# Two sums of squares taken from high and low parts, with GpSimd making square and low part, and a chunk mask added into the bias tile

## The reference

```python
def rmsnorm(x, g):
    x32 = x.astype(jnp.float32)
    y = x32 * lax.rsqrt(jnp.mean(x32 * x32, axis=-1, keepdims=True) + EPS)
    return (y * g.astype(jnp.float32)).astype(x.dtype)

def first_block(x, ...):
        xr, yr, q, k, v, ga, gb = jnp.split(p, cuts, axis=-1)
        ...
        q = head_rmsnorm(q.reshape(b_, s_, ATT_HEADS, HEAD_DIM), q_norm_g[l])
        k = head_rmsnorm(k.reshape(b_, s_, ATT_HEADS, HEAD_DIM), k_norm_g[l])
        y_b = stick_breaking_attention(q, k, v)
        mix = jax.nn.sigmoid(ga) * y_a + jax.nn.sigmoid(gb) * y_b

def chunked_rel_attention(q, k, v, rel_bias):
    ...
    s = jnp.einsum('bcqhd,bckhd->bhcqk', qc, kb).astype(jnp.float32) * (hd ** -0.5) + bias[None, :, None]
    valid = (jnp.arange(nc)[:, None] - LEFT_CHUNKS + jnp.arange(BAND)[None, :]) >= 0
    s = jnp.where(valid[None, None, :, None, :], s, jnp.finfo(jnp.float32).min)
    p = jax.nn.softmax(s, axis=-1).astype(v.dtype)
```

## Time and profile before

| | |
|---|---|
| median of 3 runs | 1972.4 us (1970.75 to 1972.7) |
| the profiled execution, its own time | 1976.53 us |
| its span, from the first instruction to the last | 1974.7 us |
| mean granted clock of TensorE | 0.99 of full |
| busy: TensorE, its weight loads | 1929.9 us, 1570.2 us |
| busy: VectorE, ScalarE, GpSimd | 944.9 us, 916.9 us, 788.6 us |

### The profile page before, as it was taken

The page is one execution under the profiler, slowest core; times in us unless marked ns, Lnnn a source line. Parts: engine busy times, 40 slices in busy tenths (PEclk is TensorE's granted clock), DMA queues, the critical chain, the costliest instruction groups (busy, mean ns, idle before and its releaser), DMA issues.

```text
span 1974.7 us, 25379 instructions
## 1 busy us (share of the span) xinstructions
PE 1929.9 (98%) x8744; PEld 1570.2 (80%) x8744; DVE 944.9 (48%) x1135; ACT 916.9 (46%) x1220; POOL 788.6 (40%) x357
## 2 busy tenths in 40 slices
PE   6999999999999999999999999999999999999998
PEld 5778777877788888888888888787777788888886
DVE  6666666666443343222434331446776553434312
ACT  5577777776555554223222222356767332222222
POOL 0133333334344444443444445543332534444443
PEclk9999999999999999999999999999999999999999
DMA  7333333333222222222222223222222222222332
GB/s 302 116 99 126 127 127 124 120 106 128 75 96 96 96 96 96 97 98 90 99 96 96 96 98 104 90 81 86 74 74 75 78 94 96 96 96 96 100 102 75
DMA packets 54617, 203.17 MB, mean 103 GB/s; under 512 B 6064, under 2 KB 6192, under 8 KB 53296
## 3 DMA queue, kind: packets, MB, share of 16 engines
q1 hardware_dynamic: 54576, 202.62, 30.4%
HBM read 200.50 MB, written 2.10 MB: 103 GB/s over the span
## 4 chain that ended last, share of the span: by engine, by line
PE 76%; issue 12%; POOL 6%; DVE 3%; ACT 2%; DMA 0%; POOLq 0%; ACTq 0%; DVEq 0%
PE bank L617 23%; PE bank L618 22%; PE bank L622 22%; POOL WL L512 5%; PE bank L1034 1%; PE bank L641 1%; DVE TG L1627 1%; PE bank L823 1%; PE bank L824 1%; PE bank L828 0%; PE bank L1072 0%; PE bank L1063 0%; PE bank L767 0%; PE bank L775 0%; ACT ARENA L1540 0%
## 5 line engine op out<-in xcount | busy, mean ns | idle before, releaser
L512 POOL TENSOR_TENSOR WL<-ring,WH 128x1024 fp32r<-128x1024 f32 (+1 forms) x318 | 765.6, 2408 | 1146.4 <-ACT WH L1159 1146.4
L1159 ACT ACTIVATE WH<-ring 128x1024 fp32r<-128x1024 f32 (+2 forms) x326 | 338.9, 1042 | 830.2 <-PE bank L622 768.3
L617 PE MATMUL bank<-HH,WL 128*128 128x512 f32 x1744 | 689.1, 395 | 8.5 <-POOL WL L512 5.2
L618 PE MATMUL bank<-HH,WH 128*128 128x512 f32 x1744 | 683.0, 392 | 0.0
L622 PE MATMUL bank<-HL,WH 128*128 128x512 f32 x1744 | 432.5, 390 | 0.8 <-DVE HL L1627 0.8
L617 PEld LDWEIGHTS bank<-HH,WL 128*128 128x128 f32 x1744 | 330.1, 189 | 79.0 <-POOL WL L512 9.1
L618 PEld LDWEIGHTS bank<-HH,WH 128*128 128x128 f32 x1744 | 330.1, 189 | 67.4
L622 PEld LDWEIGHTS bank<-HL,WH 128*128 128x128 f32 x1744 | 327.4, 188 | 70.7 <-DVE HL L1627 2.8
L617 PE MATMUL bank<-FH,WL 128*128 128x512 f32 x544 | 211.8, 389 | 0.0
L618 PE MATMUL bank<-FH,WH 128*128 128x512 f32 x544 | 211.7, 389 | 0.0
L622 PE MATMUL bank<-FL,WH 128*128 128x512 f32 x544 | 135.0, 389 | 0.0
(11 more groups left out here) (345 smaller groups left out, 2082.5 us busy)
## 6 DMA issues: line engine op xcount, KB each, us to landing
ring<-in_stream SPq DMA_DIRECT2D x355, 512.0 KB, 3.3
ARENA<-in_ada SPq DMA_DIRECT2D x8, 1024.0 KB, 13.0
ring<-in_stream SPq DMA_DIRECT2D x8, 448.0 KB, 10.5
XT<-in_xt SPq DMA_DIRECT2D x2, 1024.0 KB, 6.1
result<-XT SPq DMA_DIRECT2D x3, 512.0 KB, 2.7
result<-XT SPq DMA_DIRECT2D x2, 256.0 KB, 2.1
vec<-in_vec SPq DMA_DIRECT2D x1, 220.0 KB, 2.6
```

The source lines that it names most:

```text
L512: nc.gpsimd.tensor_tensor(WL[:, slot, 0:cols], ring[:, u % RING, 0:cols], WH[:, slot, 0:cols].bitcast(F32), ALU.subtract).then_inc(w_low, 1)
L617: mm(out_ap, part(WL, base, loc, k), xh(k), start=(start and k == 0), stop=False)
L618: mm(out_ap, part(WH, base, loc, k), xh(k), start=False, stop=False)
L1159: A(WH[:, split_at(base, loc)[1], 0:cols], ring[:, u % RING, 0:cols], ACT.Copy).then_inc(w_high, 1)
```

## The change

The change has two parts.

In the first mixer's loop ScalarE now writes the square of the next q and k as fp32r (`QSH`, `KSH`), GpSimd squares the copies `QR` and `KR` once more in full precision and subtracts the high part (`QSL`, `KSL`), and TensorE sums high and low part with a matrix of -1 in fp32r; the root takes the sign back by its scale. `square_low` stands on GpSimd behind the split of GATES (q) and behind that of XR (k). The first head's sums, ahead of the loop, stay as they were.

In the second mixer the matmuls with `chunkb` are gone. GpSimd adds -1e30 to the later chunk's 64 columns of the bias tile in the ring, for queries 0 to 63 of each block, for both heads of a pair, ahead of the split of its unit 5.

Semaphores are merged or added to fit (`dt_act` takes the place of four).

```diff
@@ gpsimd, constants
-            keep(chunkb[:, :], ALU.is_ge, 0.0, [[0, P]], -1, base=63)
-            keep(chunkb[:, :], ALU.is_ge, 0.0, [[1, P]], 0, base=-64)
@@ gpsimd, first mixer
+            def square_low(h, square, x, low, high, done):
+                nc.gpsimd.tensor_tensor(M[square], M[x], M[x], ALU.mult).then_inc(done, 1)
+                pool.wait_ge(done, 2 * h + 1)
+                nc.gpsimd.tensor_tensor(M[low], M[square], M[high].bitcast(F32), ALU.subtract).then_inc(done, 1)
+
             with pool.Fori(0, HEADS - 1) as h:
                 for loc, n in HEAD_SPLIT.items():
                     split(U_HEAD, loc, SPLIT_BEFORE[U_HEAD] + n, h, HEAD_UNITS, 8, 2 * P if loc == GATES else UNIT)
+                    if loc == GATES:
+                        pool.wait_ge(q["q_evac"], 2 * h + 4)
+                        square_low(h, "QSQ", "QR", "QSL", "QSH", q["q_sq_low"])
+                    if loc == XR:
+                        pool.wait_ge(q["k_evac"], 2 * h + 4)
+                        square_low(h, "KSQ", "KR", "KSL", "KSH", q["k_sq_low"])
@@ gpsimd, second mixer
+            def mask_bias(t):
+                u = U_PAIR + BIAS
+                pool.wait_ge(arrived[u % RING], t * (16 * PAIR_UNITS // RING) + 16 * (u // RING + 1))
+                for hh in range(2):
+                    later_keys = ring[0:64, u % RING, (hh + 1) * S - 64:(hh + 1) * S]
+                    nc.gpsimd.tensor_tensor(later_keys, later_keys, chunk_mask[0:64, :], ALU.add).then_inc(r["bias_masked"], 1)
             with pool.Fori(0, 3) as t:
                 for j, loc in rest:
+                    if loc == 5:
+                        mask_bias(t)
                     split(U_PAIR, loc, SPLIT_BEFORE[U_PAIR] + 4 + j, t, PAIR_UNITS, 7)
@@ tensor
+            def square_parts(b, high, low, low_done, n):
+                mm(bank[b][:, :], negones_r[:, :], M[high], start=True, stop=False)
+                pe.wait_ge(low_done, 2 * n)
+                return mm(bank[b][:, :], negones_r[:, :], M[low], start=False, stop=True)
...
-                q_square(h + 1)
+                square_parts(5, "QSH", "QSL", q["q_sq_low"], h + 1).then_inc(q["q_ms"], 1)
                 pe.wait_ge(q["yb_done"], h + 1)
-                k_square(h + 1)
+                square_parts(7, "KSH", "KSL", q["k_sq_low"], h + 1).then_inc(q["k_ms"], 1)
...
-                        last = mm(bank[b][:, c + w - P:c + w], identb[:, :], chunkb[:, :], start=False, stop=True,
-                                  skip_group_check=True)
@@ scalar
-                A(M["RQ"], bank[5][:, :], ACT.Sqrt, bias=eps1[:, :], scale=1.0 / P).then_inc(q["rq_done"], 1)
+                A(M["RQ"], bank[5][:, :], ACT.Sqrt, bias=eps1[:, :], scale=sign / P).then_inc(q["rq_done"], 1)
...
-                A(M["QSQ"], bank[0][:, :], ACT.Square).then_inc(q["q_evac"], 1)
+                A(M["QSH"], bank[0][:, :], ACT.Square).then_inc(q["q_evac"], 1)
@@ vector
-                        dve.wait_ge(arrived[u % RING], t * (16 * PAIR_UNITS // RING) + 16 * (u // RING + 1))
+                        dve.wait_ge(r["bias_masked"], 2 * t + 2)
```

More of the change, by code:

```diff
@@ L224, in program @@
         strictb = sb("strictb", [P, P], BF16)
-        chunkb = sb("chunkb", [P, P], BF16)
+        chunk_mask = sb("chunk_mask", [P, 64])
         SS = sb("SS", [P, S])
@@ L247, in mixer1_tiles @@
             d.update(RSQ=d["RQ"], RSK=d["RK"], A2=d["M2"], ML=d["M2"], U=d["IX"])
+            d["QSH"], d["KSH"], d["QSL"], d["KSL"] = (tile_of(ML, n) for n in range(4))
             d["QN"], d["KN"], d["VF"] = (tile_of(QKV, n) for n in range(3))
@@ L380, in program @@
         SS_BEFORE = [0] + [8 + 6 * n for n in range(N_RES - 1)]
-        names = ("q_evac k_evac v_evac v_tr xr_evac q_ms k_ms rq_done rk_done rsq rsk qn_done kn_done "
+        names = ("q_evac k_evac q_sq_low k_sq_low v_evac v_tr xr_evac q_ms k_ms rq_done rk_done rsq rsk qn_done kn_done "
                  "gy_done conv_done z_done absz_done ez_done lnp_done p_done ph_done pl_done s_done att_done pv_done "
@@ L391, in program @@
         cv_dve = sem("cv_dve")
-        names = ("bc_conv bc_tap bc_silu dt_z dt_abs dt_exp dt_ln dt_sp dt_la cs_done tr_dt tr_evac "
-                 "g_mm g_evac g_mask xs_conv xs_tap xs_silu xs_tr xd_done sel_done csb_done "
+        names = ("bc_conv bc_tap bc_silu dt_act dt_sp dt_la cs_done tr_dt tr_evac "
+                 "g_mm g_evac g_mask bias_masked xs_conv xs_tap xs_silu xs_tr xd_done sel_done csb_done "
                  "dd_done ncst ed_done mm_done y_mm y_skip z_silu yz_done yss_done q_high q_low k_high k_low v_evac v_tr pv_mm "
@@ L496, in _ @@
             for t, value in ((ones, 1.0), (negones, -1.0), (negtri, -1.0), (ident, 0.0),
-                             (identb, 0.0), (strictb, NEG), (chunkb, NEG)):
+                             (identb, 0.0), (strictb, NEG), (chunk_mask, NEG)):
                 step(nc.gpsimd.memset(t[:, :], value))
@@ L533, in lows @@
                                             ALU.subtract).then_inc(pool_low, 1)
+            M = mixer1_tiles()
+            def square_low(h, square, x, low, high, done):
+                nc.gpsimd.tensor_tensor(M[square], M[x], M[x], ALU.mult).then_inc(done, 1)
+                pool.wait_ge(done, 2 * h + 1)
+                nc.gpsimd.tensor_tensor(M[low], M[square], M[high].bitcast(F32), ALU.subtract).then_inc(done, 1)
             pool.wait_ge(w_low, KD)
@@ L576, in _ @@
                 for j, loc in rest:
+                    if loc == 5:
+                        mask_bias(t)
                     split(U_PAIR, loc, SPLIT_BEFORE[U_PAIR] + 4 + j, t, PAIR_UNITS, 7)
             for j, loc in rest:
+                if loc == 5:
+                    mask_bias(3)
                 if loc == 11:
@@ L1046, in scores @@
                                    start=(i != 0), stop=False, skip_group_check=True)
-                        mm(bank[b][:, c:c + w], N[f"QB{hh}"][:, i * P:(i + 1) * P], N[f"KA{hh}"][:, 0:w],
-                           start=False, stop=False, skip_group_check=True)
+                        last = mm(bank[b][:, c:c + w], N[f"QB{hh}"][:, i * P:(i + 1) * P], N[f"KA{hh}"][:, 0:w],
+                                  start=False, stop=True, skip_group_check=True)
                         if hh and i == 3:
                             first.then_inc(unit_done, 1)
-                        last = mm(bank[b][:, c + w - P:c + w], identb[:, :], chunkb[:, :], start=False, stop=True,
-                                  skip_group_check=True)
                     last.then_inc(r["s_mm"], 1)
@@ L1241, in _, with q_root, k_root @@
             M = mixer1_tiles()
-            def q_root(n):
+            def q_root(n, sign=-1.0):
                 act.wait_ge(q["q_ms"], n + 1)
-                A(M["RQ"], bank[5][:, :], ACT.Sqrt, bias=eps1[:, :], scale=1.0 / P).then_inc(q["rq_done"], 1)
-            def k_root(n):
+                A(M["RQ"], bank[5][:, :], ACT.Sqrt, bias=eps1[:, :], scale=sign / P).then_inc(q["rq_done"], 1)
+            def k_root(n, sign=-1.0):
                 act.wait_ge(q["k_ms"], n + 1)
-                A(M["RK"], bank[7][:, :], ACT.Sqrt, bias=eps1[:, :], scale=1.0 / P).then_inc(q["rk_done"], 1)
+                A(M["RK"], bank[7][:, :], ACT.Sqrt, bias=eps1[:, :], scale=sign / P).then_inc(q["rk_done"], 1)
             def v_turned(n):
@@ L1269, in _ @@
             A(M["SGB"], bank[1][:, :], ACT.Sigmoid).then_inc(q["sgb_done"], 1)
-            q_root(0)
-            k_root(0)
+            q_root(0, 1.0)
+            k_root(0, 1.0)
             act.wait_ge(unit_done, DONE + KD)
@@ L1325, in _ @@
                 A(M["KR"], bank[1][:, :], ACT.Copy).then_inc(q["k_evac"], 1)
-                A(M["KSQ"], bank[1][:, :], ACT.Square).then_inc(q["k_evac"], 1)
+                A(M["KSH"], bank[1][:, :], ACT.Square).then_inc(q["k_evac"], 1)
                 absolute(h)
@@ L1477, in _ @@
             weight_high(U_BC, 6)
[L1478 to L1484, removed]
+            A(N["DZ"], bank[4][:, :], ACT.Identity, bias=v("dt_bias_2")).then_inc(r["dt_act"], 1)
+            act.wait_ge(r["dt_act"], 1)
+            A(N["DE"], N["DZ"], ACT.Abs).then_inc(r["dt_act"], 1)
+            act.wait_ge(r["dt_act"], 2)
+            A(N["DE"], N["DE"], ACT.Exp, scale=-1.0).then_inc(r["dt_act"], 1)
+            act.wait_ge(r["dt_act"], 3)
+            A(N["DE"], N["DE"], ACT.Ln, bias=one[:, :]).then_inc(r["dt_act"], 1)
             def conv(a, b, loc, t, it=0):
@@ L1968, in _ @@
                     dve.wait_ge(r["bc_tap"], 3 * n + k)
-            dve.wait_ge(r["dt_ln"], 1)
+            dve.wait_ge(r["dt_act"], 4)
             STT(N["DT"], N["DZ"], zero[:, :], N["DE"], ALU.max, ALU.add).then_inc(r["dt_sp"], 1)
```

1 line of the change is left out of this document (removed).

## The result

The changed kernel takes 1974.91 us as the median of 20 runs (1970.86 to 1980.61). The kernel before, run beside it, takes 1972.28 us (20 runs, 1970.53 to 1975.09). The ratio is 1.0014, with a 95% interval of 1.0008 to 1.0020, so the change costs 2.6 us, between 1.6 and 3.9. The forecast was 1974.4 us and +2.0 us. That the two agree so closely is in part luck: three terms of the sum were off in size, and their errors mostly cancelled.

What follows compares the result with a forecast made beforehand. The prediction took TensorE, busy 98% of the span, as the bound. Its terms, -4.9 + 3.9 + 3.3 - 0.3 = +2.0 us, put the median at 1974.4 us, range 1966.8 to 1978.5.

Steps and rivals of the forecast that it cites:

- The gain of the sums: First mixer's loop: two fp32r products replace each full-precision sum on TensorE, saving 0.81 us a head, 4.9 us over six.
- the last pass keeps nothing: Last of seven loop passes: its gain is lost because TensorE waits 0.7 us for VectorE's HL parts of the output projection.
- V's low half in heads 2 to 7: GpSimd's squares and VectorE's turns end V's split at 12.3 to 12.4 us, due 11.71; loss 6 x 0.55 = 3.3 us.
- The first head: The fourth row of `ada_rows` ends later, V's load goes out at 94.4, and TensorE's wait for V grows: +3.9 us.
- The clock: TensorE's granted-clock dip behind the first head's wait for V moves with that wait; 1.7 us either way in the range.
- The second mixer: Score products without mask matmuls save 3 to 4 us if all kept; waits swallow most, leaving -0.3 us.
- the turns cost more: Rival: GpSimd's exchanges with VectorE before V's split cost 0.55 us each, not 0.43, adding 3.4 us: 1977.8; chance 0.12.

Runs made afterwards that it cites:

- the squares moved: The changed kernel with both squares and both subtractions on GpSimd behind V's split instead of behind GATES' and XR's: 1969.04 us, ratio 0.9988 to the kernel before.
- masks only: The changed kernel with the first mixer's squares taken back and the second mixer's mask part kept: 1971.20 us, ratio 0.9994 to the kernel before.
- squares only: The changed kernel with the mask part taken back and the first mixer's squares kept: 1974.48 us, ratio 1.0016 to the kernel before.
- V's load ahead on the kernel before: The kernel before the change, with SyncE's load of V issued ahead of ADA3's and nothing else: 1966.68 us, ratio 0.9980.
- the third product: Extra 128x512 GpSimd product ahead of k's square: changed kernel 1982.12 us; with squares behind V's split and V's load ahead of ADA3's, 1970.91 us.

## Why the forecast came out right, by its steps

- **The gain of the sums**: 0.81 us a head forecast, 0.79 in the rows, 0.81 by the head's period with the squares moved. Right. That the last pass keeps nothing was right to 0.2 us, but by another wait: the one for ScalarE's `HH` takes 0.6 us back, not the one for `HL`. With the squares moved both stand there (0.6 us more, and 0.7 where the kernel with masks only has none), and so the pass loses more than it gains.
- **V's low half in heads 2 to 7**: mechanism and end right (12.19, forecast 12.3 to 12.4), size too high. The step that failed is "V, due at 11.71, 0.6 to 0.7" late: it is 0.48 by that count, because a square takes 1.04 us and not 1.27, and three exchanges of 0.55, 0.45 and 0.32 us come in place of four of 0.43. The fourth falls into the 0.65 us in which GpSimd waits for ScalarE's copy of XR in any case. Most of the loss sits at XR (0.44 us, forecast 0.3), little at V. By the heads' periods the loss is 0.45 us (49.92 against 49.47) where the forecast had 0.65.
- **The first head**: the issue of V's load was right (94.06, forecast 94.4). The step that failed is "+3.9 us": I moved the landing by as much as the issue. The load took 6.15 us from issue to ScalarE's start in the execution that I read and 4.63 us in the changed kernel; its issue took 1.32 us there and 0.33 here. In the two other kernels in which this load goes out at 90.4, the issue took 1.25 and 1.13 us and the load 5.1 and 5.4. The wait ended 2.0 us later against the execution that I read. Against the profile of the kernel with masks only, which has the same first mixer and waits 4.1 us there, it ended 3.2 us later. With the squares moved it is 4.3 us, so the one execution that I read had a wait about 1 us longer than these two.
- **The clock**: forecast as moving with the wait, 1.7 us either way. It did not only move. Over all runs the mean granted clock is 0.9909 in the kernel before (33 runs) and 0.9908 with masks only, but 0.9890 in the changed kernel (20) and 0.9891 with squares only. A difference of 0.0019 of 1973 us is up to 3.7 us of TensorE's time, less where it idles anyway. With the squares moved it is 0.9899, which is up to 2 us. Matched with masks only, that kernel is 6.1 us ahead when the loop ends and 2.9 at the end: 1.3 us go in the waits for `HH` and `HL`, and 1.6 in a stretch at 1.2 GHz from 905.8 on that the other execution lacks. That is what it lacks against the sum. With V's load ahead on the kernel before it is 0.9923.
- **The second mixer**: -0.3 forecast, -0.4 in the matched trace. Right, and by the waits that were named.

Set together against the kernel with masks only, the loop and the first head make +1.15 us by the matched matmuls (+0.55 at the end of the loop, 0.60 behind it), the masks -0.4. That is +0.8, and of the measured 1.6 to 3.9 us it leaves 1 to 3. The matched starts hold every wait up to there. Behind it the changed kernel's profiled execution loses another 3.7 us to that with masks only, 3.2 of it in two stretches at 1.2 GHz, from 913.2 and from 1609.5 on. In both windows the granted clock is 1.00 with masks only, and 0.72 in the changed kernel, with TensorE busy throughout:

```profile
912.00:918.00 6.00, 6.00 (x20) 4.73 (x20) 0.18 (x1) 0.20 (x1) 0.86 (x1) 0.72 0.27 87
1608.00:1614.00 6.00, 6.00 (x28) 5.14 (x28) 0.18 (x1) 0.61 (x3) 2.35 (x1) 0.72 0.26 96
```

The first of the two stands in the kernel before as well (from 912.9 on), so one execution proves nothing here; it is the means above that differ, and they have the size for what is left. Why the squares bring more time at 1.2 GHz, beyond the longer stretch behind the first head's wait, was not tried and stays open. The forecast of +2.0 had the first mixer 1 us too high and left this out.

The rival "the turns cost more" falls: they cost 0.32 to 0.55 us, 1.3 a head in all, where 1.7 was forecast. The Trainium skill (SBUF — State Buffer, section "SBUF: two separate sides") has the blocked side go on some 115 ns behind the other's end, measured there on a DMA of GpSimd's queue behind a copy on VectorE. No run here shows that: GpSimd's instructions, by their bare durations, must have started 0.13 us ahead of the recorded end of VectorE's (196.61 against 196.74 at XR's split), as in the earlier trace rows.

## What to carry to other kernels

Work given to an engine that is idle most of the time costs by its place: ask when the next thing that it makes is due, and how much room that leaves. If two engines hold each other off, count the room of both, as the third product shows. And before pricing a late load by its issue, look at what stands ahead of it in its queue: here swapping two loads gave 4.4 us. The change as first made cost 2.6 us; with its squares behind V's split it gave 0.4 to 4.1, and 4.2 by the medians once the loads were swapped.

## What was not expected of the hardware

- A product of a 128x512 tile with itself took GpSimd 1.04 us, one of two tiles 1.27 us, a subtraction with fp32r output 1.28 to 1.30 us.
- In nine of the traces TensorE waited 3.3 to 7.1 us near 95 us, and in eight of them a stretch at 1.2 GHz of 3.4 to 10.2 us began within 1 us behind the wait's end or up to 5 us ahead of it; where the wait was 0.6 us or less there was none, and the last trace had one of 3.4 us behind a wait of 1.8. The load swapped in the kernel before took away a wait of 4 to 5 us and gained 4.4 us by the medians.
